# Latent attention: plain query columns of two heads in one block, rotary query columns made once and kept in DRAM, squares summed by two-column products

## The reference

```python
q = (_rms(c_q, mla_q_norm[j]) @ mla_w_q_up[j]).reshape(b, s, N_MLA_HEADS, MLA_QK)
kv = (_rms(c_kv, mla_kv_norm[j]) @ mla_w_kv_up[j]).reshape(b, s, N_MLA_HEADS, MLA_NOPE + MLA_V)
k_rope_h = jnp.broadcast_to(k_rope[:, :, None, :], (b, s, N_MLA_HEADS, MLA_ROPE))
k = jnp.concatenate([kv[..., :MLA_NOPE], k_rope_h], axis=-1)
v = kv[..., MLA_NOPE:]
q = _rms(q, mla_g_qn[j])
k = _rms(k, mla_g_kn[j])
q = jnp.concatenate([q[..., :MLA_NOPE], _rope(q[..., MLA_NOPE:], positions)], -1)
k = jnp.concatenate([k[..., :MLA_NOPE], _rope(k[..., MLA_NOPE:], positions)], -1)
o = _causal_softmax_attn(q.transpose(0, 2, 1, 3), k.transpose(0, 2, 1, 3), v.transpose(0, 2, 1, 3))
```

## Time and profile before

| | |
|---|---|
| median of 3 executions | 2633.2 us (2623.6 to 2635.95) |
| the profiled execution, its own time | 2625.39 us |
| its span from the first to the last instruction | 2623.7 us |
| busy share PE, DVE, ACT, POOL | 96%, 66%, 50%, 42% |
| mean granted clock of PE | 0.986 of full speed |
| opening of the latent heads | 1480.4 to 1521.4 us of the span |
| five turns with preparation, then one without | to about 1840.4 us, then to about 1883 us |

### The profile page before, as it was taken

The page is one execution under the profiler, slowest core; times in us unless marked ns, Lnnn a source line. Parts: engine busy times, 40 slices in busy tenths (PEclk is TensorE's granted clock), DMA queues, the critical chain, the costliest instruction groups (busy, mean ns, idle before and its releaser), DMA issues. The chain is left out here.

```text
span 2623.7 us, 37082 instructions
## 1 busy us (share of the span) xinstructions
PE 2510.2 (96%) x12000; PEld 2041.3 (78%) x12000; DVE 1739.9 (66%) x2659; ACT 1312.3 (50%) x2483; POOL 1112.8 (42%) x839
## 2 busy tenths in 40 slices
PE   7989999989999999999988999999799999999999
PEld 5767777667788888888777777778687888888887
DVE  6667787855766666478654377777648665665495
ACT  6566777745433333444654366666545333333443
POOL 2034554311466566555311432332003665565554
PEclk9999999999999999999999999999899999999999
DMA  4111110153223232664302000000242323234843
GB/s 145 45 29 33 33 33 9 33 177 112 81 102 106 96 116 84 238 235 149 103 23 57 14 20 22 21 21 21 88 161 91 117 100 104 100 112 141 287 126 117
DMA packets 182795, 242.74 MB, mean 93 GB/s; under 512 B 31376, under 2 KB 105872, under 8 KB 182672
## 3 DMA queue, kind: packets, MB, share of 16 engines
q1 hardware_dynamic: 182672, 241.19, 27.6%
HBM read 175.60 MB, written 65.54 MB: 92 GB/s over the span
## 5 line engine op out<-in xcount | busy, mean ns | idle before, releaser
L2374 POOL TENSOR_TENSOR l0s_run_lo<-l0s_run,l0s_run_hi 128x512 fp32r<-128x512 f32 (+2 forms) x120 | 143.4, 1195 | 216.0 <-DVE l0s_run_hi L2527 216.0
L471 POOL TENSOR_TENSOR l1f_wd_lo<-l1f_d,l1f_wd_hi 128x512 fp32r<-128x512 f32 x77 | 107.9, 1402 | 105.6 <-ACT l1f_wd_hi L546 105.6
L471 POOL TENSOR_TENSOR l0f_wd_lo<-l0f_d,l0f_wd_hi 128x512 fp32r<-128x512 f32 x77 | 110.1, 1431 | 96.5 <-ACT l0f_wd_hi L546 96.4
L84 PE MATMUL banks<-l0f_T_hi,l0f_op_hi 128*128 128x512 f32 x352 | 137.2, 390 | 1.3 <-DVE l0f_T_lo L691 1.3
L84 PE MATMUL banks<-l1f_T_hi,l1f_op_hi 128*128 128x512 f32 x352 | 137.2, 390 | 1.3 <-DVE l1f_T_lo L691 1.3
L86 PE MATMUL banks<-l1f_T_hi,l1f_op_lo 128*128 128x512 f32 x352 | 137.0, 389 | 0.0
L86 PE MATMUL banks<-l0f_T_hi,l0f_op_lo 128*128 128x512 f32 x352 | 137.0, 389 | 0.0
L85 PE MATMUL banks<-l1f_T_lo,l1f_op_hi 128*128 128x512 f32 x352 | 136.9, 389 | 0.0
L85 PE MATMUL banks<-l0f_T_lo,l0f_op_hi 128*128 128x512 f32 x352 | 136.9, 389 | 0.0
L433 POOL TENSOR_TENSOR l1f_s<-l1f_raw 128x512 f32<-128x512 f32 x44 | 66.7, 1516 | 155.9 <-DMA l1f_raw<-in_w_ffn_gu_dram 134.3
L503 ACT ACTIVATE l1f_op_hi<-l1f_s 128x512 fp32r<-128x512 f32 x88 | 55.2, 632 | 140.4 <-PE banks L86 140.4
(11 more groups left out here) (534 smaller groups left out, 8371.6 us busy)
## 6 DMA issues: line engine op xcount, KB each, us to landing
l0f_raw<-in_w_ffn_gu_dram SPq DMA_DIRECT2D x22, 1024.0 KB, 5.0
l1f_raw<-in_w_ffn_gu_dram SPq DMA_DIRECT2D x22, 1024.0 KB, 5.0
l0f_a_raw<-hidden_rows SPq DMA_DIRECT2D x77, 256.0 KB, 3.9
l1f_a_raw<-hidden_rows SPq DMA_DIRECT2D x77, 256.0 KB, 3.6
hidden_rows<-l0f_hid SPq DMA_DIRECT2D x44, 256.0 KB, 2.0
l0f_d<-in_w_ffn_down_dram SPq DMA_DIRECT2D x44, 256.0 KB, 5.1
hidden_rows<-l1f_hid SPq DMA_DIRECT2D x44, 256.0 KB, 2.0
l1f_d<-in_w_ffn_down_dram SPq DMA_DIRECT2D x44, 256.0 KB, 4.9
```

What stands on the lines that cost most here:

```text
L84: pe.matmul(out, l_hi, r_hi, start=first, stop=False, skip_group_check=True)
L471: pool.tensor_tensor(wd_lo[g % RING][:], held[HELD_AT[DOWN[p][1]]][i][:], as_f32(wd_hi[g % RING][:]), ALU.subtract).then_inc(wd_lo_done, 1)
L2374: pool.tensor_tensor(run_lo[x % NR][:, f:HALF], run[x % NR][:, f:HALF], as_f32(run_hi[x % NR][:, f:HALF]), ALU.subtract).then_inc(run_spli ...
```

## The change

Three things change in `latent_heads`.

1. The plain query columns (64 of each head) of both heads of a pair stand in one block of 128 columns. A unit `q half part` now serves both heads, so that a pair has two units of 18 products and not four. ACT squares the block and copies the upper 64 rows as the plain rows of head 1, DVE scales the lower 64 for head 0, both by the gains.
2. The rotary columns of all 12 heads are made once, in the opening: three blocks of four heads (`rope b half`), 18 products for each block and half, 108 in all. DVE multiplies each by a table of cosines and by one of sines, and the results go to DRAM. In each turn SP loads the rotary rows of the next pair from there into the query tile, three DMAs for each head. The tables are first spread over the partitions by 12 DMAs.
3. Squares are summed by products in which 128 columns of squares are the stationary operand and a matrix of 2 (or 4) columns of ones and zeros the moving one. The result has the query rows in partitions at once, so that the copy by ACT and the four transposes fall away (`rq` has no part on PE any more). The sums of the rotary columns are made once in the opening (`rss`), kept in DRAM and loaded for each pair (`base`).

With them `OPENING`, `extras` and the order of POOL are written anew, and SP's order in a turn is now: rotary rows of head 0, base, weights, store, a wait for the last score row of the turn, rotary rows of head 1, three stores.

```diff
-    OPENING = ["kv 0", "kv 1", "kv 2", "kv 3", "q 0 0", "ksum 0", "q 0 1", "q 0 2", "knorm 0", "q 1 0", "q 1 1",
-               "wk", "ksum 1", "q 1 2", "kturn 0", "ss 0", "knorm 1", "rq 0", "qnorm 0", "S", "S", "q 2 0", "q 2 1",
-               "S", "kturn 1", "wq 0", "q 2 2", "q 3 0", "S", "S", "q 3 1", "S", "q 3 2", "S", "kturn 2", "ss 1",
-               "wq 1", "rq 1", "kturn 3", "S", "v0", "qnorm 1"]
-    extras = {0: ["q 0 0", "q 0 1"], 1: ["v1", "q 0 2"], 3: ["kv 0"], 4: ["kv 1"], 5: ["kv 2", "ksum 0"],
-              6: ["kv 3", "knorm 0", "wk"], 7: ["q 1 0", "ksum 1", "q 1 1", "q 1 2", "knorm 1"], 8: ["ss 0"],
-              9: ["rq 0"], 10: ["kturn 0"], 11: ["kturn 1"], 12: ["qnorm 0", "q 2 0", "wq 0"], 13: ["q 2 1", "v0"], 15: ["q 2 2"],
-              16: ["q 3 0"], 17: ["q 3 1", "q 3 2"], 18: ["wq 1", "kturn 2"], 19: ["ss 1"],
-              20: ["rq 1", "qnorm 1"], 21: ["kturn 3"]}
+    OPENING = ["kv 0", "kv 1", "kv 2", "kv 3", "wr 1", "rope 0 0", "ksum 0", "rope 0 1", "knorm 0", "rss 0 0", "q 0 0", "ksum 1",
+               "q 0 1", "rss 0 1", "q 0 2", "knorm 1", "ss 0", "kturn 0", "wr 2", "q 1 0", "rq 0", "q 1 1", "qhi 0", "qnorm 0", "q 1 2",
+               "kturn 1", "ss 1", "rope 1 0", "S", "qhi 1", "rq 1", "S", "rope 1 1", "qnorm 1", "S", "rss 1 0", "kturn 2", "S",
+               "rope 2 0", "qhi 2", "rss 1 1", "S", "kturn 3", "S", "rope 2 1", "qhi 3", "rss 2 0", "S", "wq", "wk", "rss 2 1", "S", "v0"]
+    extras = {1: ["v1"], 2: ["kv 0"], 3: ["kv 1"], 4: ["kv 2", "ksum 0"], 5: ["kv 3", "knorm 0", "wk"], 6: ["ksum 1"],
+              7: ["knorm 1", "q 0 0"], 8: ["q 0 1"], 9: ["q 0 2"], 10: ["qhi 0", "ss 0"], 11: ["rq 0", "kturn 0"],
+              12: ["qnorm 0", "kturn 1"], 13: ["q 1 0", "v0"], 14: ["q 1 1"], 15: ["q 1 2"], 16: ["qhi 1", "ss 1", "wq"],
+              17: ["rq 1", "qnorm 1", "kturn 2"], 18: ["qhi 2"], 19: ["kturn 3"], 20: ["qhi 3"]}
...
+            def load_rotary(h, g):
+                for first, kind, row, n in ((HD, 0, 0, ROPE), (HD + ROPE, 1, H, H), (HD + ROPE + H, 1, 0, H)):
+                    sp.dma_start(q32[first:first + n, h, :], rope_dram[kind, bass.ds(g * 2 * ROPE + h * ROPE + row, n), :]).then_inc(rope_in[h], 16)
...
+            spread_table()
             sp.wait_ge(made_ones, 1)
             with nc.allow_non_contiguous_dma("gains"):
                 sp.dma_start(gcol[0:NOPE, 0:1], g_k[0:NOPE].unsqueeze(1)).then_inc(g_in, 16)
+                for h in range(2):
+                    sp.dma_start(gq[h * HD:(h + 1) * HD, 0:1], g_q[0:NOPE].unsqueeze(1)).then_inc(g_in, 16)
+            load_rotary_weights(1)
+            sp.wait_ge(wr_lo, 1)
+            load_rotary_weights(2)
             load(1)
+            store_rotary(0)
+            store_rotary(1)
...
+            def turn(g, last=False):
+                sp.wait_ge(at_.scores_made, at_.ns * g + at_.ns // 2)
+                load_rotary(0, g + 1)
+                sp.wait_ge(q_read, 2 * g + 2)
+                load_base(g + 1)
+                if not last:
+                    load(g + 2)
+                at_.store_job(sp, 0, g)
+                sp.wait_ge(at_.scores_made, at_.ns * g + at_.ns)
+                load_rotary(1, g + 1)
+                for n in range(1, 4):
+                    at_.store_job(sp, n, g)
...
                 elif kind == "q" and n[1] == "2":
+                    act.wait_ge(q_made, 2 * g + half + 1)
...
+                    act.activation(q_sq[half][:], bank_of(unit, g)[:], ACT.Square).then_inc(q_squared, 1)
+                    act.activation(q32[LOW, 1, columns(half)], bank_of(unit, g)[HIGH, :], ACT.Copy, scale=gq[HIGH, 0:1]).then_inc(q_scaled[1], 1)
+                elif kind == "qhi":
+                    act.wait_ge(rope_in[h], 48 * (g + 1))
+                    act.wait_ge(q_scaled[h], 2 * g + half + 1)
+                    act.activation(qt["hi"][:, h, columns(half)], q32[:, h, columns(half)], ACT.Copy).then_inc(q_hi, 1)
...
                 elif kind == "ss":
-                    h = int(n[0])
-                    act.wait_ge(ss_made, 2 * g + h + 1)
-                    act.activation(q_sq[0][:], bank_of(what, g)[:], ACT.Copy).then_inc(ss_out, 1)
...
+                    for i in range(HT):
+                        last = pe.matmul(bank_of(what, g)[:, 2 * i:2 * i + 2], q_sq[half][:, i * P:(i + 1) * P], twos[:],
                                          start=True, stop=True, skip_group_check=True)
                     last.then_inc(ss_made, 1)
-                elif kind == "rq":
-                    h = int(n[0])
-                    free(what, g)
-                    pe.wait_ge(ss_out, 2 * g + h + 1)
-                    for i in range(4):
-                        last = pe.transpose(bank_of(what, g)[:, i * P:(i + 1) * P], q_sq[0][:, i * P:(i + 1) * P], k["ident"][:])
-                    last.then_inc(ss_turned, 1)
...
+            for s in range(2):
+                pe.wait_ge(rope_stored[s], 96)
```

More of the change, by code:

```diff
@@ L40 @@
 X_AT = 228864 - NS * D * 4
[L41 to L42 removed]
+OPENING_AT = WORK_AT + 116 * 1024
+OPENING_END = OPENING_AT + 12 * 1024
 class Memory:
@@ new lines, in load_base, with store_rotary, spread_table @@
+            def load_base(g):
+                sp.dma_start(base[:].rearrange("p a h i -> p (a h i)"), base_dram[:, bass.ds(g * G, G)]).then_inc(base_in, 16)
+            def store_rotary(r):
+                b, half = ROPES[r]
+                sp.wait_ge(rope_copied, r + 1)
+                for kind in range(2):
+                    sp.dma_start(rope_dram[kind, b * P:(b + 1) * P, columns(half)], rope_out[kind][r % 2][:]).then_inc(rope_stored[r % 2], 16)
+            def spread_table():
+                for n in range(4):
+                    for kind, row, first, count in ((0, HD, 0, ROPE), (1, HD + ROPE + H, 0, H), (1, HD + ROPE, H, H)):
+                        at_row = n * ROPE + first
+                        sp.dma_start(tables[kind][at_row:at_row + count, :], table[row:row + count, :]).then_inc(spread, 16)
```

319 lines of the change are left out of this document (203 added, 116 removed).

## The result

The changed kernel took 2692.9 us (median of four runs, 2691.8 to 2693.8) where the kernel before took 2632.1 (four runs, 2623.6 to 2636.0): 1.0227 times as long, 95% interval 1.0211 to 1.0243. It is slower by 61 us; the forecast was 2634, with 2612 to 2652 as its range. The profiled execution took 2693.8 us.

What follows compares the result with a forecast made beforehand. PE, 96% busy, was taken to pace only parts of a turn, DVE or hand-over waits the others. Five turns -26, opening +22 and clock +5 made +1: 2634 us, range 2612 to 2652.

Steps and rivals of the forecast that it cites:

- The hole: Tau 0 and 1: PE waits there for DVE's `pt_lo` anyway, so the query unit costs nearly nothing and removing it gains nearly nothing.
- the clock: Five turns: half clock may follow the uncovered idle time at tau 0 and 1; two falls of five at 2.5, +5 us.
- Rival 2: Slower by the clock: it falls in all five turns and once in the opening, +16, 2649 us; chance 0.15.
- Tau 7 to 11: `rq` and a `kturn` leave, `ss` is shorter, PE's idle 1.2 us mostly goes: 13.6 us, a gain of 1.9.
- tau 12 to 15: A `kturn` comes in and steps wait for reads of the one bank: 10.3 us, a loss of 1.0.
- Tau 16 to 1: Two parts where query units leave PE and DVE becomes fuller: 11.5 and 11.3 us, gains of 2.4 and 1.9.
- The opening: First `kv` product to first T: PE gains rotary products, +20.0 us of work, and more waiting: +22, bounds +17 and +30.
- wait for gains: Opening: ACT's first copy waits for gains issued behind 12 table DMAs, leaving PE idle for 3 us.
- two-column products: Sums of squares by the new way, four products with two moving columns: priced at 0.85 us, bounds 0.45 and 1.08.
- Rival 3: A load is late: ACT stands at `wk` or `qhi` 2 us in each turn, +10, 2644 us; chance 0.10.
- Rival 1: PE paces everything, so time falls by what PE loses: 28 us, to 2605; chance 0.27.
- 2 to 6: Tau 2 to 6 of a turn: the four `kv` units come one block earlier, nothing removed; no gain, 11.9 us.

Runs made afterwards that it cites:

- experiment 4: Kernel before the change, with the first query unit of every turn cut from 18 products to 3: 2642.1 us, ratio 1.0046.
- experiment 5: Changed kernel with extra unused products in three idle stretches of each turn, to keep the clock up, waits left as they are: 2680.8 us, ratio 1.0191.
- experiment 1: Changed kernel with the read of the sums (`rq 0`, `rq 1`) asked for one block earlier: 2682.8 us, ratio 1.0206.
- experiment 7: Changed kernel with the same steps in another order (keys' blocks and reads of sums earlier) and the gains loaded first: 2657.6 us, ratio 1.0100.
- experiment 10: Changed kernel, steps reordered and gains first, with more moved forward (second sums and their read in tau 15, key turns in 16 and 18): 2658.5 us, ratio 1.0121.
- experiment 11: Changed kernel with 3 of 18 products in each of the opening's six rotary blocks, the other 15 left out: 2685.7 us.
- experiment 6: Changed kernel with sums read one block earlier and extra unused products in tau 0 and 1 and ahead of `kturn 2`: 2680.5 us, ratio 1.0180.

## Why the prediction was wrong

**The hole and the clock: mechanism right, size wrong.** The query products in tau 0 and 1 cost nothing, as I had said (experiment 4: a turn of 63.85 us with the cut, 63.8 without). Taking them away uncovers the hole in every turn, and the clock fell at it in all five, where I counted two of five at 2.5 us. With the two waits it fell two or three times in a turn. Keeping it up brought 3.0 us a turn and 14 in the five (experiment 5), for my 5, and that is net of what the extra products cost. Rival 2 had that term at 20 and still ended at 2649, because it kept the other terms of my sum.

**Tau 7 to 11: the failed price.** I wrote that PE's idle time "mostly goes" and took 13.6; it was 17.6. A wait for the one bank was priced, but in tau 12 to 15 (1.0 us), and its source was misjudged: the sums' read is 0.17 us long and stands behind 3 us of VectorE's work in its own block. Moving the read brought 14.9 (experiment 1). Moving all steps brought 13.2 (experiment 7), but that part then holds six query products less and a key turn more, so it is no like-for-like check of my 13.6. For tau 12 to 15 I took 10.3; it was 11.9, of which a part is the clock (11.4 with it up).

**Tau 16 to 1: the failed step.** I let both parts shrink to VectorE's busy time with a little on top: 22.8 us for 27.1, of which 21.1 busy and 1.7 waiting. VectorE's busy time was forecast well (20.75 measured), but its waiting did not go with TensorE's work: it was 5.3 us before, 6.4 after, and 5.2 or more in every version. So 27.15 came, 4.4 us over in each turn, 22 in all. A part of the 4.4 is the clock's (0.86 in this stretch): at full clock it took 26.9 with 1.0 us of extra products in it (experiment 5), so about 3 of the 4.4 stay without the clock, an estimate from these two. The stretch could be made shorter, 24.75 us in most turns of experiment 10, but only with work moved out into tau 12 to 15, which grew by 2.0. A stretch whose fullest remaining engine is idle for 5 of 27 us, at full clock, is not bound by any one engine; I read the busy time of the fullest engine as a floor that would be reached.

**The opening: right for the size, partly by luck.** +25.2 for +22. PE's idle time came as forecast (5.9 us for 6), though the wait for gains was 4.6 and not 3. Its busy time was 60.3 and not 56.8 (36.8 and my 20.0): 0.9 of that is two-column products at 1.00 and not 0.85, and the opening had about 9 us at half clock for 3 before, a term that my sum did not have. Experiment 11 shows that the working (products simply add) holds only while TensorE is behind everything else there.

**The rest.** 5.2 us came before the stage, 3.9 of them before the first product of the second layer, which the change does not touch. They are most likely not the change's: in other traces of the changed kernel with the same code up to there, the first `kv` product came at 1481.0 (experiment 11) to 1489.5 us (experiment 1), and in traces of the kernel before at 1480.4 to 1486.2. Rival 3 was wrong: ScalarE's waits in the five turns name no DMA, and the query weights in rows of 256 bytes landed 2.8 us after their issue (192 KB; 288 KB took 3.3 before). Rival 1 (TensorE paces all) is refuted for tau 0 and 1 by experiment 4, and as a whole by the result.

Per turn: +4.4 for tau 16 to 1, +4.0 for 7 to 11, +2.7 for 2 to 6, +1.5 for 12 to 15 over the forecast 58.6 (the clock's 1.0 a turn stood outside it) make the 71.2. No run has one of the three changes alone, so what each of them is worth by itself stays open.

## What to carry to other kernels

Where an engine is 95% busy, first cut some of its work in one place and look at the turn: in the kernel before, 3.4 us less of matmuls in a hole made the turn not shorter but, through the clock, longer. A part of a loop that no engine fills is held by hand-overs, so count those, and do not book the waits in it as a gain when work leaves: here VectorE waited 5 to 7 us in one such part of a turn in all 18 kernels, whatever work was in it. When steps share one bank, look where the short read that frees it stands in the other engine's queue; 0.17 us of work held TensorE for 3 to 4.

## What the runs showed of the hardware

**VectorE held up while GpSimd works.** In the timeline of VectorE above, the 128x1 `nmx` takes 0.94 us, where the same instruction takes 0.16 at 1660.23, and a row scaling of 640 columns takes 1.25 (0.55 in the first experiment, for the same shape and place). GpSimd at that time:

```profile
1656.35 1.28 POOL L3152 TENSOR_TENSOR l1a_qt_lo<-l1a_q,l1a_qt_hi 128x512 fp32r<-128x512 f32 x1 [4.76 <-ACT l1a_qt_hi L3244]
1657.58 1.27 POOL L3126 TENSOR_TENSOR l1a_wk_lo<-l1a_wk_raw,l1a_wk_hi 128x512 fp32r<-128x512 f32 x1
```

The `nmx` ends at 1657.64, as GpSimd's first subtraction does (1657.63); the maximum and `pt_lo`, which read PSUM, are not longer than elsewhere. So up to 1.5 us of the 3.2 that TensorE waited there come from this. The Trainium skill, "GPSIMD Engine Reference", section "8. Key points", says that the two engines contend where VectorE's instruction has two SBUF inputs or a two-port mode; the trace agrees. No run here took GpSimd's work away, so the 1.5 us are read, not tested.

**The same idle span, with and without a fall.** 2.04 us of idle time at tau 13 left the clock at 1.00 in four turns of experiment 1 and went with 0.50 in the same four turns of experiment 6. In the changed kernel itself 3.21 us ahead of `kturn 0` were followed by 0.50 in the turn shown, and 3.20 us in the next two turns by none, while the hole at tau 2 (2.70 us, 6.7 in the first turn) and that of about 4.1 us ahead of `kturn 2` went with a fall in every turn. In experiment 4 four of five turns fell at the hole of tau 2. What decides it was not settled.
